# State-space kernel products on four column blocks, and a reordered latent-attention round

## The reference, cut to what matters

```python
proj = h @ w_in
u_s, z_s, q_lat, kv_lat, k_rope, z_m, gl_s, gl_m = split(proj)
y_s = ssm_branch(u_s, ...)            # 64 groups of 16 channels, 64 complex states each
glu_a, glu_b = split(gelu(y_s) @ w_glu + b_glu)
y_s = ((glu_a * sigmoid(glu_b)) * silu(z_s)) @ w_br_ssm
y_m = mla_branch(q_lat, kv_lat, k_rope, positions, ...)   # 16 heads, q/k 64 + 32 rotary, v 64
y_m = (y_m * silu(z_m)) @ w_br_mla
merged = sigmoid(gl_s) * y_s + sigmoid(gl_m) * y_m
out = merged @ w_out
```

## Time and profile before

| | |
|---|---|
| median of 3 runs | 1881.41 us (1881.14 to 1885.5) |
| profiled execution, its own time | 1882.79 us |
| its span | 1881.0 us |
| mean granted TensorE clock | 0.977 of full speed |
| busy share of the span | TensorE 96%, VectorE 54%, ScalarE 48%, GpSimd 19% |
| chain that ended last | TensorE 68%, VectorE 12%, ScalarE 8%, issue 7%, DMA 4% |

### The profile page before, as it was taken

How to read it: one execution, slowest core, us unless ns; L and a number is a source line. 1 busy time by engine, 2 the same in 40 slices (tenths; PEclk the granted TensorE clock), 3 DMA queues, 4 the chain that set the end, 5 groups by cost and what they waited for, 6 DMA issues and landing times.

```text
span 1881.0 us, 31207 instructions
## 1 busy us (share of the span) xinstructions
PE 1800.0 (96%) x11925; PEld 1609.3 (86%) x11925; DVE 1017.0 (54%) x1506; ACT 899.3 (48%) x1190; POOL 353.0 (19%) x520
## 2 busy tenths in 40 slices
PE   6899999999999999899999998999999999899996
PEld 6899999999999998799998886888777777788885
DVE  3455565555433347785654326466576776744443
ACT  4567666666533344333333223356556556633332
POOL 0011110111000005988800981000000000000001
PEclk9999999999999998899999997999999999999998
DMA  3221222222222345343333542765211211223432
GB/s 114 84 78 56 89 67 78 89 69 68 77 90 89 89 147 147 106 130 100 123 100 109 142 140 80 231 192 135 72 62 51 90 61 50 89 90 112 129 95 101
DMA packets 68034, 189.11 MB, mean 101 GB/s; under 512 B 15284, under 2 KB 19572, under 8 KB 67832
## 3 DMA queue, kind: packets, MB, share of 16 engines
q1 hardware_dynamic: 64040, 176.04, 30.1%
q0 software_dynamic: 3920, 12.06, 2.3%
HBM read 165.76 MB, written 19.95 MB: 99 GB/s over the span
## 4 chain that ended last, share of the span: by engine, by line
PE 68%; DVE 12%; ACT 8%; issue 7%; DMA 4%; POOL 1%; SPq 0%; DVEq 0%; ACTq 0%
PE J L846 24%; PE J L1104 17%; PE J L858 7%; PE J L1075 6%; DMA WR<-weights 4%; DVE WL L1813 2%; PE Z L896 2%; PE J L1265 2%; POOL E L2464 1%; ACT E L1417 1%; ACT E L1413 1%; ACT WH L1345 1%; PE Z L950 1%; PE Z L918 1%; DVE Q2L L1817 1%
## 5 line engine op out<-in xcount | busy, mean ns | idle before, releaser
L1813 DVE TENSOR_TENSOR WL<-WR,WH 128x1024 fp32r<-128x1024 f32 x271 | 354.7, 1310 | 311.2 <-ACT WH L1345 302.2
L1345 ACT ACTIVATE WH<-WR 128x1024 fp32r<-128x1024 f32 x271 | 285.5, 1054 | 222.0 <-DMA WR<-weights 104.5
L846 PE MATMUL J<-XH,WH 128*128 128x264 f32 (+1 forms) x1376 | 286.3, 290 | 18.4 <-DVE XL L1817 10.9
L846 PE MATMUL J<-XL,WH 128*128 128x264 f32 (+1 forms) x1376 | 280.8, 286 | 0.0
L846 PE MATMUL J<-XH,WL 128*128 128x264 f32 (+1 forms) x1376 | 280.5, 285 | 0.0
L846 PEld LDWEIGHTS J<-XH,WH 128*128 128x128 f32 x1376 | 216.9, 191 | 25.3 <-issue 8.8
L846 PEld LDWEIGHTS J<-XL,WH 128*128 128x128 f32 x1376 | 215.9, 191 | 0.0
L846 PEld LDWEIGHTS J<-XH,WL 128*128 128x128 f32 x1376 | 214.9, 191 | 0.0
L2464 POOL TENSOR_SCALAR_AFFINE_SELECT E<-E 128x128 f32<-128x128 f32 (+1 forms) x160 | 51.9, 363 | 448.5 <-DVE E L1895 240.8
L2482 POOL TENSOR_TENSOR SA<-SQ 128x512 f32<-128x512 f32 (+1 forms) x3 | 3.9, 1315 | 694.5 <-ACT SQ L1599 504.0
L1104 PE MATMUL J<-X2H,WH 128*128 128x512 f32 x168 | 68.4, 407 | 4.1 <-DVE X2L L2188 4.1
(11 more groups left out here) (438 smaller groups left out, 4291.3 us busy)
## 6 DMA issues: line engine op xcount, KB each, us to landing
WR<-weights SPq DMA_DIRECT2D x271, 512.0 KB, 3.5
CPS<-cp_dram SPq DMA_DIRECT2D x8, 576.0 KB, 6.2
cp_dram<-CQR POOLq DMA_DIRECT2D x16, 144.0 KB, 2.9
cp_dram<-CQI POOLq DMA_DIRECT2D x16, 144.0 KB, 2.7
X<-tokens SPq DMA_DIRECT2D x4, 528.0 KB, 6.0
H<-tokens SPq DMA_DIRECT2D x8, 264.0 KB, 3.9
bp_dram<-BQR POOLq DMA_DIRECT2D x8, 256.0 KB, 2.4
bp_dram<-BQI POOLq DMA_DIRECT2D x8, 256.0 KB, 2.3
```

The source lines that it names most:

```text
L846: mm = pe.matmul(o[:, 512 * h:512 * h + half], ws[:, s, w], xs[:, a:a + half], start=(k == 0 and i == 0), stop=(k == 7 and i == 2))
L1345: act.activation(WH[:, n % SPLIT, :], WR[:, n % RAW, :], ACT.Copy).then_inc(w_hi, 1)
L1813: dve.tensor_tensor(WL[:, n % SPLIT, :], WR[:, n % RAW, :], WH[:, n % SPLIT, :].bitcast(F32), ALU.subtract).then_inc(w_lo, 1)
```

## The change

The kernel products of a state-space block go to four column blocks: group g = 4 * half + c is written to partitions 32c to 32c + 15, columns 128 * half on, first four products, then the four skip terms. The eviction to GS becomes four ACTIVATEs of 16 x 256. In an attention round, the gate 0 weights take job n+1 and the z_m weights job n+2; gate 0 is finished ahead of the scores and z_m one u later; gate 1's k steps are dealt out as 1, 3, 2, 2. ScalarE splits at the start (n+2), after K2H (n+3), after V2H (n+4) and at u = 3 (n+5); VectorE splits n+2 after the rotary sum, n+3 after K2L, n+4 at u = 4 and n+5 at u = 5. Silu moves from the head of u = 4 to the end of u = 5, the copy to GST from u = 5 to behind the loop. The split of N_LAT+7 ahead of the rounds falls into the first round, and that of N_GLU+2 behind the YGH and YGL pieces.

```diff
@@ -781,10 +781,10 @@
 
             def attend(m):
                 load_row(N_ATT + 4 * m, ROW_ATT + 2 * m)
-                load_row(N_ATT + 4 * m + 1, ROW_ATT + 2 * m + 1)
+                load_row(N_ATT + 4 * m + 1, ROW_MERGE + 4 * m)
                 if positive(m):
                     store_gate(m - 1)
-                load_row(N_ATT + 4 * m + 2, ROW_MERGE + 4 * m)
+                load_row(N_ATT + 4 * m + 2, ROW_ATT + 2 * m + 1)
                 load_row(N_ATT + 4 * m + 3, ROW_MERGE + 4 * m + 1)
 
             repeat(sp, DT, 1, attend)
@@ -1131,13 +1131,15 @@
                 if m == 0:
                     pe.wait_ge(dd_ready, 2)
                     pe.wait_ge(bb_landed, 16)
-                for g in range(GT):
-                    at = 512 * (g % 2) + P * (g // 2)
-                    pe.matmul(J[(t + 1) % 2][0:GP, at:at + P], BBS[:, GT * m + g],
-                              CPS[m % 3][:, g, 0:SUB].rearrange("p i q -> p (i q)"),
-                              start=True, stop=False, skip_group_check=True)
-                    mm = pe.matmul(J[(t + 1) % 2][0:GP, at:at + GP], IDENT[:, 0:GP], DD[:, GT * m + g],
-                                   start=False, stop=True, skip_group_check=True)
+                for half in range(GT // 4):
+                    for c in range(4):
+                        g = 4 * half + c
+                        pe.matmul(J[(t + 1) % 2][32 * c:32 * c + GP, P * half:P * (half + 1)], BBS[:, GT * m + g],
+                                  CPS[m % 3][:, g, 0:SUB].rearrange("p i q -> p (i q)"),
+                                  start=True, stop=False, skip_group_check=True)
+                    for c in range(4):
+                        mm = pe.matmul(J[(t + 1) % 2][32 * c:32 * c + GP, P * half:P * half + GP], IDENT[:, 0:GP],
+                                       DD[:, GT * m + 4 * half + c], start=False, stop=True, skip_group_check=True)
                 mm.then_inc(g_done, 1)
 
                 pe.wait_ge(read_out[slot(t)], nth(t) + 1)
@@ -1207,13 +1209,13 @@
 
                     o = J[j][:, 512:512 + S2]
                     if first == 0:
-                        pe.wait_ge(w_lo, val(n + 3 + j))
+                        pe.wait_ge(w_lo, val(n + 2 + 2 * j))
                         if positive(2 * m - 1 + j):
                             pe.wait_ge(raw_gate, val(2 * m - 1 + j))
                     for k in range(first, last):
                         w = slice(k * P, (k + 1) * P)
                         for i, (ws, xs) in enumerate(((WH, X2H), (WH, X2L), (WL, X2H))):
-                            mm = pe.matmul(o, ws[:, (n + 2 + j) % SPLIT, w], xs[:, k * S2:(k + 1) * S2],
+                            mm = pe.matmul(o, ws[:, (n + 1 + 2 * j) % SPLIT, w], xs[:, k * S2:(k + 1) * S2],
                                            start=(k == 0 and i == 0), stop=(k == 7 and i == 2))
                     if last == 8:
                         mm.then_inc(job_done, 1)
@@ -1236,6 +1238,7 @@
                 up(2, t + 2, LKH, LKL).then_inc(up_done, 1)
                 gate(0, 2, 7)
                 up(3, t + 3, LKH, LKL).then_inc(job_done, 1)
+                gate(0, 7, 8)
 
                 def score(u):
 
@@ -1286,25 +1289,23 @@
                     for k in range(first, last):
                         w = slice(k * P, (k + 1) * P)
                         for i, (ws, xs) in enumerate(((WH, X2H), (WH, X2L), (WL, X2H))):
-                            mm = pe.matmul(J[(t + 5) % 2][:, 0:S2], ws[:, (n + 1) % SPLIT, w],
+                            mm = pe.matmul(J[(t + 5) % 2][:, 0:S2], ws[:, (n + 2) % SPLIT, w],
                                            xs[:, k * S2:(k + 1) * S2],
                                            start=(k == 0 and i == 0), stop=(k == 7 and i == 2))
                     if last == 8:
                         mm.then_inc(job_done, 1)
 
                 pe.wait_ge(read_out[slot(t + 5)], nth(t + 5))
-                pe.wait_ge(w_lo, val(n + 2))
+                pe.wait_ge(w_lo, val(n + 3))
                 z_m(0, 3)
                 for u in range(8):
                     if u + 2 < 8:
                         score(u + 2)
                     turn_weights(u)
-                    if u < 3:
-                        z_m((3, 5, 6)[u], (5, 6, 8)[u])
-                    if u == 3:
-                        gate(0, 7, 8)
+                    if u < 4:
+                        z_m((3, 5, 6, 7)[u], (5, 6, 7, 8)[u])
                     if u >= 4:
-                        gate(1, (0, 1, 4, 7)[u - 4], (1, 4, 7, 8)[u - 4])
+                        gate(1, (0, 1, 4, 6)[u - 4], (1, 4, 6, 8)[u - 4])
                     if u == 4:
                         values2(0)
                 values2(1)
@@ -1621,9 +1622,11 @@
                 act.wait_ge(g_done, val(m + 1))
                 if positive(16 * SUB * m):
                     act.wait_ge(tk_landed, val(16 * SUB * m))
-                act.activation(GS[:].rearrange("p (r x n) -> p x r n", x=2, n=P),
-                               J[(t + 1) % 2][0:GP, :].rearrange("p (x r n) -> p x r n", x=2, n=P), ACT.Copy)\
-                   .then_inc(read_out[(t + 1) % 2], 1)
+                gs = GS[:].rearrange("p (r c n) -> p c r n", c=4, n=P)
+                for c in range(4):
+                    ins = act.activation(gs[:, c], J[(t + 1) % 2][32 * c:32 * c + GP, 0:2 * P]
+                                         .rearrange("p (r n) -> p r n", n=P), ACT.Copy)
+                ins.then_inc(read_out[(t + 1) % 2], 1)
 
             for m in range(DT):
                 if m == DT - 1:
@@ -1670,7 +1673,6 @@
                     root(5, S2)
             for k in range(4):
                 if k == LATT:
-                    split_hi(N_LAT + 7)
                     act.wait_ge(pattern, 6)
                     for x in range(2):
                         act.activation(Q2H[x][96:P], PAT[96:P, 0], ACT.Copy)
@@ -1689,7 +1691,7 @@
 
             def attend(m):
                 n, t, h = N_ATT + 4 * m, T_ATT + 8 * m, 2 * m
-                split_hi(n + 3)
+                split_hi(n + 2)
                 act.wait_ge(rope_ready, val(m + 2))
                 if positive(8 * m):
                     act.wait_ge(s_done, val(8 * m))
@@ -1702,6 +1704,7 @@
                 for x in range(2):
                     mm = act.activation(K2H[x][0:64], J[t % 2][64 * x:64 * x + 64, 0:S2], ACT.Copy)
                 mm.then_inc(k_hi, 1)
+                split_hi(n + 3)
 
                 src = result2(n, t + 3)
                 act.activation(R2[:], src, ACT.Copy).then_inc(read_out[(t + 3) % 2], 1)
@@ -1733,24 +1736,22 @@
                 act.activation(V2H[:], J[(t + 4) % 2][:, 0:S2], ACT.Copy).then_inc(v2_hi, 1)
                 split_hi(n + 4)
                 for u in range(8):
-                    if u == 4:
-                        src = result2(n + 1, t + 5)
+                    weights_hi(u)
+                    if u + 2 < 8:
+                        exponent(u + 2)
+                    if u == 3:
+                        split_hi(n + 5)
+                    if u == 5:
+                        src = result2(n + 2, t + 5)
                         if positive(2 * m):
                             act.wait_ge(om_ready, val(2 * m))
                         act.activation(VZ[:], src, ACT.Silu).then_inc(read_out[(t + 5) % 2], 1)
-                    weights_hi(u)
-                    if u + 2 < 8:
-                        exponent(u + 2)
-                    if u == 4:
-                        split_hi(n + 5)
-                    if u == 5:
-                        act.wait_ge(job_done, val(n + 3))
-                        if positive(m):
-                            act.wait_ge(gate_stored, val(16 * m))
-                        act.activation(GST[:], J[0][:, 512:512 + S2], ACT.Copy).then_inc(raw_gate, 1)
+                act.wait_ge(job_done, val(n + 2))
+                if positive(m):
+                    act.wait_ge(gate_stored, val(16 * m))
+                act.activation(GST[:], J[0][:, 512:512 + S2], ACT.Copy).then_inc(raw_gate, 1)
                 act.wait_ge(job_done, val(n + 4))
                 act.activation(SGM[:, cols(m * S2, S2)], J[1][:, 512:512 + S2], ACT.Copy).then_inc(raw_gate, 1)
-                split_hi(n + 6)
 
             repeat(act, DT, 2, attend)
 
@@ -1758,6 +1759,7 @@
             for m in range(DT):
                 s = slice(m * S2, (m + 1) * S2)
                 act.activation(YGH[:, s], YG[:, s], ACT.Copy).then_inc(yg_hi, 1)
+            split_hi(N_GLU + 2)
 
             def glu(m):
                 n, t = N_GLU + 2 * m, T_GLU + 2 * m
@@ -2302,7 +2304,6 @@
             dve.nop().then_inc(read_out[(T_LAT + 4) % 2], 1)
             latent(LATT, rooted(6, S2))
             dve.tensor_tensor(RO[0:64], RO[0:64], R2[0:64], ALU.add).then_inc(rope_ready, 1)
-            split_lo(N_LAT + 7)
             dve.wait_ge(rope_hi, 2)
             for x in range(2):
                 ins = low(K2L[x][64:96], RO[0:32], K2H[x][64:96])
@@ -2318,6 +2319,7 @@
```

(8 more changed lines are left out.)

## The result

The changed kernel took 1869.66 us, the median of four runs (1865.62 to 1871.62); the kernel before, on the same chip, 1881.46 (1881.14 to 1885.5, four runs). The ratio is 0.9931 with an interval of 0.9915 to 0.9946: 13 us faster, 10 to 16 (11.8 by the two medians). Forecast were 1869 and a range of 1862 to 1877.

What follows compares the result with a forecast made beforehand. TensorE, busy 96% of the span, bounds the kernel. Terms -8.0 - 3.2 + 0.5 - 1.8 = -12.5 us took the profiled 1882.79 us to 1870.3, as a median 1869; range 1862 to 1877.

Steps and rivals of the forecast that it cites:

- Part 1: State-space stage: kernel products on four column blocks save 1.0 us in each of eight blocks, -8.0 us (-8.8 to 0).
- The cap by BT: State-space block: L1149 can't start before ScalarE has emptied BT, so at most 1.0 us per block is saved.
- The bound of 1.36 from L1178: Kernel products: upper limit of 1.36 us per stretch from L1178 and L1149's pace, half of it below; 1.2 taken.
- The rule against it: Kernel products: weight loads overlap matmuls in flight only when the row group differs, so column blocks give nothing, 8.0 us poorer.
- Rival A: State-space kernel products: column blocks don't overlap, all rows of the array being in use; 1877 us, chance 0.08.
- C: Kernel products: every change of column block waits for the previous matmul to drain, +2.1 us per block; 1894 us, chance 0.05.
- Rounds: Attention rounds: reordered splits and jobs give -0.65 + 0.2 in each of seven rounds, -3.2 us (-5.6 to +1.8).
- Front: Round up to first value product: VectorE split leaves (-1.23), Exp table load after R2's copy adds 0.60; -0.65 us taken.
- Tail: Round from first to second value product: table load out, two VectorE splits in; +0.2 us (0 to +0.5).
- First round: First attention round: longer gap and lower clock cost 1.5 us, the later part saves 1.0; net +0.5 (-1.0 to +1.6).
- GLU: Into the GLU: split moved behind the copies, -1.35, plus about a third of the slow stretch's 1.4; -1.8 us.
- Costs set at nothing: Four GS evictions, later loads on SyncE's queue (margin 0.4 us before rotary Q2H) and the moved GLU split: 0 each.

Runs made afterwards that it cites:

- y_first: Changed kernel with the outputs' first product moved between the kernel products and the states' product that reads BT; 1865.95 us, ratio 0.991 to the kernel before.
- two_blocks: Changed kernel with the kernel products on two column blocks (partitions 0 and 64) and two evictions of 16x512; 1865.15 us in a single run.
- gap_split: Changed kernel with VectorE's split of n+4 ahead of that step's PTL instead of behind it; 1862.06 us, ratio 0.9895 to the kernel before.
- glu_back: Changed kernel with the split of N_GLU+2 back ahead of the YGH and YGL copies; 1872.32 us, ratio 0.9929 to the kernel before.
- pairwise: Changed kernel, still four column blocks, with product and skip term of a block issued together; 1865.51 us in a single run.
- all: Changed kernel with the edits of y_first, gap_split, prefetch and fill together; 1855.13 us, ratio 0.9852 to the kernel before.
- silu_back: Changed kernel with only ScalarE's Silu back at u == 4, ahead of that step's weights_hi; 1867.48 us, ratio 0.9913 to the kernel before.
- prefetch: Changed kernel with a one-column Exp on scratch right behind R2's copy; 1864.25 us, ratio 0.9909 to the kernel before.
- fill: Changed kernel with five k steps of gate 0 instead of two ahead of the first round's third product, all eight ahead of the fourth; 1866.57 us, ratio 0.9908.

## Why the prediction was right, and where it wasn't

The median is right to 0.7 us. The terms are off by more, in both directions, and that their sum came so close is in part luck: the stages give -14.1 us for the -12.5 forecast. In order:

- **Part 1, -8.0 forecast, -7.6 measured.** The cap by BT was the step that carried it, and it held: 1.18 us for the 1.25 forecast, six times; *y_first* shows that it is a cap, and *two_blocks* that two column blocks are already enough to reach it. Mis-sized below the cap: I took 1.2 us for the 16 products, they take 0.56 to 0.65, about a quarter of 2.24, while two blocks take 1.08. The bound of 1.36 from L1178 was for two blocks, and its half was near the right value for four; I stayed near the upper end. Both cases I had left out are there: the third block reached 1.76 because ScalarE's BT stood behind YG, 0.6 us more than the others, and the first took 0.86, 0.3 less, but stood 0.8 us for another wait where it was 0.6 before.
- **The rule against it.** The trace overlaps them: 16 matmuls with all 128 rows in 0.56 us. By the Trainium skill (TensorE: Matmul & The Clock Gate, Part 3, The mechanism) weight loads overlap matmuls in flight only when the row group differs; here the row group is the same throughout, only the output columns differ, and the measurement decides against the rule as it is worded. That part 1 would give nothing was my reading of it, and more than Part 3 says: its table under Measured speedup vs the span model has three column tiles at 2.38 times the speed. Another page, TensorEngine Tiling (Array Packing), Performance Considerations, has four-fold column tiling for a stationary operand with a free dimension of 32; with 16 columns it was 2.24/0.56 = 4.0 here by the pace of the halves, and 2.24/0.65 = 3.4 to the next product. Rival A is out, and so is C: no change of block costs a drain.
- **Rounds, -3.2 forecast for seven, -5.3 measured.** Front, from R2's copy to the first value product: -0.65 forecast, measured -0.93 in four rounds (12.22 for 13.15) and -0.1 in three, -0.57 on the mean: near the forecast, but by two errors that cancel. The split did leave the chain: with Silu put back the front is 1.3 us shorter than before, for the split's 1.23. The load costs 0.4 us where it runs ahead of the wait, not 0.6; in the third, fifth and seventh round it costs 1.3. The step that failed is "it can start when R2 is copied", which holds in four of the seven rounds. Tail: +0.2 forecast, -0.05 measured (9.65 for 9.71): the load's leaving gives 0.93, and the rest of the reordered tail takes 0.87, which I put down to the two splits (the k steps dealt out anew lie in it too, and weren't tried alone). The mis-sized terms are these, and the wait for the last PB, 0.45 us for about 1. The chain named for it (VectorE, last PB) is right by the new wait and by *gap_split*. The rest no term had: from a round's start to R2 it takes 10.48 us for 10.63, seven times; which edit did that was not tried.
- **First round, +0.5 forecast, -0.1 measured.** The gap grew to 3.68 us as said, and the slow stretch lies behind it as said (about eight matmuls at 0.63). Up to R2's copy the round is 1.44 us longer, for 1.5 forecast. What the later part gives back was 1.5 us from R2 to the value product (13.71 to 12.22), not 1.0. In three other profiles of the same round (*glu_back*, *pairwise*, *y_first*) the slow stretch lasts 6.8 us for 3.4 and the round takes 41.1 to 41.2 us, +1.1. Of the nine profiles with this opening four have the shorter stretch and five the longer, so -0.1 is the luckier half.
- **GLU, -1.8 forecast, -1.05 measured.** The wait fell from 3.04 to 1.99 us (the other 1.1 of the eighth round's -2.2 are its front and start, counted above), 1.05 for the 1.35 forecast. The step that failed is the third of the slow stretch, -0.45: it stayed whole, and the GLU took 175.8 us before and after. *glu_back* prices the split's place at 2.5 us once the rounds are shorter.
- **Costs set at nothing.** Four GS evictions take 1.53 us; the waits for TK in *y_first* and *all* don't come from them: TK's transfers were issued 0.6 to 6.5 us after GS was complete. The round's opening split does wait for its landing, 3.5 to 3.8 us in six rounds, and rotary Q2H behind it still stands 0.7 to 0.9 for RO, more than the margin of 0.4. In the seventh round the split waits 4.9 us and Q2H follows it without a gap, so the margin was used up there; that round is as long as the third and the fifth.
- **Median and profile.** Stages and median part here: -14.1 by the stages, -11.8 by the medians. I take the lower-clock stretches to be the difference (mean clock 0.977 in the profiled run, 0.974 to 0.975 in the other three); this is argued, since which stretches these were in runs without a profile was not shown.

## What to carry to other kernels

When work that hides an eviction gets shorter, price it by the eviction's end, not by the work: here a shortening of 1.6 us a block paid 1.06 until other work was put between. In a chain that two engines pass back and forth, a load or a split is worth only what of it stands in the chain; place it where its engine waits anyway, and check each copy of an unrolled loop by itself, since a table load can come at another place in one of them, as here in every first copy. With a kernel at 96% on one engine, read such changes by stage: the spread between runs was as large as the smaller terms.

## What was not expected of the hardware

- Sixteen fp32 matmuls with 16-column weights, on four column blocks, took 0.56 us by the pace of their halves (0.65 to the next product), for 2.24 on one and 1.08 on two.
- ScalarE's table load of 1.28 us ran ahead of the semaphore wait in the rounds written out straight and in the second round of the loop body (0.62 us behind R2's copy), and behind the wait in the first round of the body (1.54 us): 0.9 us of TensorE's time, three times. That the loop's head is the reason is argued from where it falls, not shown; the Trainium skill (ScalarE activation tables: per-element evaluation and per-set limits, Table sets in the compiler and the runtime) has the loads placed block by block, which fits it. The same page's 1283 ns for a load (What a function is on this engine) agree with the 1.28 us here.
- An idle gap of the same length (1.99 us before the GLU) was followed by the lower clock in the changed kernel and five of the experiments, and by none in *silu_back*, *prefetch*, *fill* and *all* (1.99 us too): about 1.6 us of the GLU's time (175.8 and 174.2), which the gap alone doesn't decide. In the first round the clock fell in all nine profiles with the changed opening, and stayed at its upper level in the two with a shorter gap (*fill*, *all*: 1.64 us for 3.68).
